# Hybrid decoder trunk on one core: the first two weight units run side by side over halves of the tokens, with smaller first loads, zero matmuls and a later sum of squares

## The reference

```python
def swiglu(x, w1, w3, w2):
    return (jax.nn.silu(x @ w1) * (x @ w3)) @ w2

def block(x, ...):
    x = x + 0.5 * rmsnorm(swiglu(rmsnorm(x, norm_g[0]), ffn1_w1, ffn1_w3, ffn1_w2), norm_g[1])
    mo, st = mixer(rmsnorm(x, norm_g[2]), w_in, ...)
    x = x + rmsnorm(mo, norm_g[3])
    x = x + 0.5 * rmsnorm(swiglu(rmsnorm(x, norm_g[4]), ffn2_w1, ffn2_w3, ffn2_w2), norm_g[5])
    return x, st
```

## Time and profile before

| | us |
|---|---|
| median of 3 runs | 1116.31 |
| lowest and highest of the 3 | 1115.22 and 1117.57 |
| the profiled execution's own time | 1118.76 |
| span of the profiled execution | 1116.7 |
| PE (matmul) busy | 1082.8 (97%) |
| PEld (weight load) busy | 1069.9 (96%) |
| DVE busy | 537.7 (48%) |
| ACT busy | 339.2 (30%) |
| POOL busy | 104.7 (9%) |
| mean granted TensorE clock | 0.985 of full speed |

### The profile page before, as it was taken

How to read it: one execution, slowest core, us unless ns; L and a number is a source line. 1 busy time by engine, 2 the same in 40 slices (tenths; PEclk the granted TensorE clock), 3 DMA queues, 4 the chain that set the end, 5 groups by cost and what they waited for, 6 DMA issues and landing times.

```text
span 1116.7 us, 21526 instructions
## 1 busy us (share of the span) xinstructions
PE 1082.8 (97%) x8929; PEld 1069.9 (96%) x8929; DVE 537.7 (48%) x942; ACT 339.2 (30%) x477; POOL 104.7 (9%) x175
## 2 busy tenths in 40 slices
PE   6999999999999999999999889999999999999995
PEld 6999999999999999998999789999999999999995
DVE  5534523433333369864546857844323334323346
ACT  5322213221222345411532333442212222113231
POOL 0000625910000000420001020000000000000000
PEclk9999999999999999999999989999999999999998
DMA  6222223233222240132312335122232232232232
GB/s 232 83 88 94 78 92 95 75 94 91 80 80 90 71 138 23 57 92 78 114 60 77 12 83 200 37 78 91 79 94 83 87 94 81 89 94 78 82 85 81
DMA packets 31921, 97.97 MB, mean 88 GB/s; under 512 B 5880, under 2 KB 8184, under 8 KB 31864
## 3 DMA queue, kind: packets, MB, share of 16 engines
q1 hardware_dynamic: 31864, 97.17, 28.8%
HBM read 92.46 MB, written 4.70 MB: 87 GB/s over the span
## 4 chain that ended last, share of the span: by engine, by line
PE 90%; DVE 6%; ACT 2%; DMA 1%; issue 1%; SPq 0%; DVEq 0%; ACTq 0%
PE ps L1855 76%; PE ps L1880 5%; PE ps L2283 2%; PE ps L1946 2%; DMA raw<-w 1%; PE ps L1892 1%; DVE x L1090 1%; PE ps L1887 1%; DVE y L1086 1%; DVE wl L896 1%; ACT wh L485 1%; PE ps L2134 0%; DVE xl L1095 0%; DVE xl L1509 0%; PE ps L2093 0%
## 5 line engine op out<-in xcount | busy, mean ns | idle before, releaser
L896 DVE TENSOR_TENSOR wl<-raw,wh 128x1024 fp32r<-128x1024 f32 (+1 forms) x149 | 183.1, 1229 | 467.5 <-ACT wh L485 467.2
L1855 PE MATMUL ps<-xh,wh 128*128 128x272 f32 x1680 | 350.9, 290 | 11.0 <-DVE xl L1005 10.8
L1855 PE MATMUL ps<-xl,wh 128*128 128x272 f32 x1680 | 348.4, 289 | 0.0
L1855 PE MATMUL ps<-xh,wl 128*128 128x272 f32 x1680 | 347.2, 288 | 0.0
L485 ACT CAST wh<-raw 128x1024 fp32r<-128x1024 f32 (+1 forms) x149 | 154.7, 1039 | 448.0 <-PE ps L1855 440.9
L1855 PEld LDWEIGHTS ps<-xh,wh 128*128 128x128 f32 x1680 | 264.3, 189 | 12.5 <-issue 11.7
L1855 PEld LDWEIGHTS ps<-xl,wh 128*128 128x128 f32 x1680 | 265.5, 189 | 0.0
L1855 PEld LDWEIGHTS ps<-xh,wl 128*128 128x128 f32 x1680 | 264.3, 189 | 0.0
L1855 PE MATMUL ps<-hh,wh 128*128 128x272 f32 x608 | 126.3, 289 | 0.5 <-DVE hl L917 0.5
L1855 PE MATMUL ps<-hl,wh 128*128 128x272 f32 x608 | 125.4, 287 | 0.0
L1855 PE MATMUL ps<-hh,wl 128*128 128x272 f32 x608 | 125.3, 287 | 0.0
(11 more groups left out here) (444 smaller groups left out, 1098.5 us busy)
## 6 DMA issues: line engine op xcount, KB each, us to landing
raw<-w SPq DMA_DIRECT2D x120, 512.0 KB, 3.5
raw<-win SPq DMA_DIRECT2D x25, 512.0 KB, 3.6
raw<-w SPq DMA_DIRECT2D x16, 384.0 KB, 3.1
raw<-wout SPq DMA_DIRECT2D x8, 512.0 KB, 3.6
x<-xT SPq DMA_DIRECT2D x4, 544.0 KB, 6.1
o_yT<-x SPq DMA_DIRECT2D x16, 136.0 KB, 1.7
cs<-cT SPq DMA_DIRECT2D x4, 516.0 KB, 4.5
o_sC<-cs SPq DMA_DIRECT2D x4, 516.0 KB, 6.8
```

The source lines that it names most:

```text
L896: V.tensor_tensor(wl[par][:, 0:cols], raw[par][:, 0:cols], wh[par][:, 0:cols].bitcast(F32), ALU.subtract).then_inc(split_done, 1)
L1855: last = mm(ps[:, bank + s, 0:HALF], w[:, kk * P:(kk + 1) * P], a[:, kk, s * HALF:(s + 1) * HALF], start=(kk == 0 and i == 0), stop=(kk == ...
```

## The change

- **Loads.** The first halves of units 0 and 1 (blocks `kk` 0 to 3), then their second halves, are loads of their own, of 128 x 512. `x` comes in six parts that keep the two halves of the tokens apart: block 0, block 1, blocks 2 and 3, blocks 4 to 7 of the first 272 tokens, then blocks 0 to 3 and 4 to 7 of the second. The first half of unit 0 is issued first. Units 2 and 3 are now loaded before the loop, and the further parameters (`prm`, `cst2`, `bst`) come after them, so behind SP's waits for the low parts of units 0 and 1.
- **ACT and DVE.** High and low parts are taken piece by piece, in the order in which the pieces are used. The table for the square root is loaded before the first cast.
- **PE, units 0 and 1.** `first_pair` replaces two calls of `up`: for the first half of the tokens, for each `kk`, three matmuls of unit 0 and three of unit 1; then the same for the second half.
- **PE, zeros.** Four matmuls of 128 x 272 on the cleared buffer `cbd`, in plain 32-bit, stand before that and wait only for the clearing.
- **Squares and sums.** On ACT the eight squares stand behind the cast of unit 2, on DVE the adds behind its low part. On PE the sums move from behind unit 1 to the first block of unit 3, and the spread from before the fourth block of unit 2 to before the third block of unit 3.

```diff
+X_PARTS = ((0, 0, 1), (0, 1, 2), (0, 2, 4), (0, 4, 8), (1, 0, 4), (1, 4, 8))
+X_WITH = ((0, 1, 2, 2, 3, 3, 3, 3), (4, 4, 4, 4, 5, 5, 5, 5))
...
+            first(0, 0, first_in[0])
             spe.dma_start(prm[:, gains], A["prm"][:, gains]).then_inc(gain_in, 16)
-            spe.dma_start(x[:, 0:2], A["xT"][:, 0:2]).then_inc(x_in[0], 16)
-            load(0, 0, A["w13_0"][0])
-            for i in range(1, 4):
-                spe.dma_start(x[:, 2 * i:2 * i + 2], A["xT"][:, 2 * i:2 * i + 2]).then_inc(x_in[i], 16)
-                if i == 1:
-                    spe.dma_start(cst[:], A["cst"]).then_inc(cst_in, 16)
-            load(1, 1, A["w13_0"][1])
+            x_part(0)
+            x_part(1)
+            first(1, 0, first_in[1])
+            x_part(2)
+            first(0, 1, raw_full[0])
+            first(1, 1, raw_full[1])
+            x_part(3)
+            x_part(4)
+            x_part(5)
+            spe.dma_start(cst[:], A["cst"]).then_inc(cst_in, 16)
+            load(2, 0, A["w13_0"][2])
+            load(3, 1, A["w13_0"][3])
...
                     elif f == 0:
-                        split(u0, u0 % 2, half(0))
-                        inputs(lambda: split(u0 + 1, (u0 + 1) % 2, half(1)))
+                        inputs()
                         split(u0 + 2, u0 % 2, half(2))
+                        for kk in range(KD):
+                            input_square(kk)
+                        split(u0 + 3, (u0 + 1) % 2, half(3))
                         input_root(0)
-                        split(u0 + 3, (u0 + 1) % 2, half(3))
                         input_copy(0, bcs[:])
...
                     elif f == 0:
-                        lo_part(u0, u0 % 2)
                         inputs()
-                        lo_part(u0 + 1, (u0 + 1) % 2)
+                        lo_part(u0 + 2, u0 % 2)
                         sum_squares(0)
-                        lo_part(u0 + 2, u0 % 2)
+                        lo_part(u0 + 3, (u0 + 1) % 2)
                         input_scale(0)
-                        lo_part(u0 + 3, (u0 + 1) % 2)
                         dve.wait_ge(r_copied, 1)
...
+            def first_pair():
+
+                for s in range(2):
+                    for kk in range(KD):
+                        pe.wait_ge(xl_ready, KD * s + kk + 1)
+                        for c in range(2):
+                            if s == 0 and kk == 0:
+                                pe.wait_ge(first_lo, c + 1)
+                            if s == 0 and kk == KD // 2:
+                                pe.wait_ge(split_done, c + 3)
+                            for i, (w, a) in enumerate(((wh, xh), (wh, xl), (wl, xh))):
+                                ins = mm(ps[:, 2 * c + s, 0:HALF], w[c][:, kk * P:(kk + 1) * P], a[:, kk, part(s)],
+                                         start=(kk == 0 and i == 0), stop=(kk == KD - 1 and i == 2))
+                            if s == 1 and kk == KD - 1:
+                                ins.then_inc(unit_used, 1)
...
-                        up(u0, hb, 0, lambda kk: pe.wait_ge(xl_ready, 2 * kk + 2))
-                        up(u0, hb, 1)
-                        input_sums(KD)
-                        up(u0, hb, 2, lambda kk: input_spread(0) if kk == 3 else None)
-                        up(u0, hb, 3)
+                        first_pair()
+                        up(u0, hb, 2)
+                        pe.wait_ge(cst_in, 16)
+                        up(u0, hb, 3, lambda kk: input_sums(KD) if kk == 0 else input_spread(0) if kk == 2 else None)
...
-            pe.wait_ge(cst_in, 16)
+            pe.wait_ge(warm_in, 1)
+            zeros = cbd[:].rearrange("p n j c -> p (n j c)")
+            for n in range(4):
+                mm(ps[:, 7, 0:HALF], zeros[:, 0:P], zeros[:, P:P + HALF], start=True, stop=True)
             ffn(0, 0, 0, 0)
```

More of the change, by code:

```diff
@@ L323, in build @@
         prm_in = sem("prm_in")
-        x_in = [sem(f"x_in{i}") for i in range(4)]
+        warm_in = sem("warm_in")
+        first_in = [sem(f"first_in{i}") for i in range(2)]
+        first_hi = sem("first_hi")
+        first_lo = sem("first_lo")
+        x_in = [sem(f"x_in{i}") for i in range(len(X_PARTS))]
         cs_in = sem("cs_in")
@@ L604, in input_square, with first_cast, inputs @@
                 nc.scalar.activation(sq_slot(kk), x[:, kk], ACT.Square).then_inc(xsq_ready, 1)
-            def inputs(between):
-                for kk in range(KD):
-                    x_loaded(kk)
-                    nc.scalar.activation(xh[:, kk], x[:, kk], ACT.Copy, scale=norm_g[:, 0, kk:kk + 1]).then_inc(xh_ready, 2)
-                between()
-                for kk in range(KD):
-                    input_square(kk)
+            def first_cast(u, z, full, done):
+                act.wait_ge(full, 16)
+                cut = slice(z * UNIT // 2, (z + 1) * UNIT // 2)
+                nc.scalar.copy(wh[u][:, cut], raw[u][:, cut]).then_inc(done, 1)
+            def inputs():
+                act.wait_ge(split_done, 2)
+                sqrt_table()
+                first_cast(0, 0, first_in[0], first_hi)
+                act.wait_ge(gain_in, 16)
+                for h in range(2):
+                    for kk in range(KD):
+                        act.wait_ge(x_in[X_WITH[h][kk]], 16)
+                        nc.scalar.activation(xh[:, kk, part(h)], x[:, kk, part(h)], ACT.Copy, scale=norm_g[:, 0, kk:kk + 1])\
+                            .then_inc(xh_ready, 1)
+                        if h == 0 and kk == 0:
+                            first_cast(1, 0, first_in[1], first_hi)
+                        if h == 0 and kk == 3:
+                            first_cast(0, 1, raw_full[0], hi_done)
+                            first_cast(1, 1, raw_full[1], hi_done)
             def input_root(stage):
@@ L1230, in s5_scalars @@
                     V.reciprocal(par(IDEN), par(S0)).then_inc(s5_par, 1)
-            def x_loaded(kk):
-                if kk == 0:
-                    dve.wait_ge(gain_in, 16)
-                dve.wait_ge(x_in[kk // 2], 16)
             def ffn1_inputs():
                 settle()
-                for kk in range(KD):
-                    x_loaded(kk)
-                    input_lo(kk)
+                first_low(0, 0, first_hi, 1, first_lo)
+                dve.wait_ge(gain_in, 16)
+                for h in range(2):
+                    for kk in range(KD):
+                        dve.wait_ge(x_in[X_WITH[h][kk]], 16)
+                        input_lo(h, kk)
+                        if h == 0 and kk == 0:
+                            first_low(1, 0, first_hi, 2, first_lo)
+                        if h == 0 and kk == 3:
+                            first_low(0, 1, hi_done, 1, split_done)
+                            first_low(1, 1, hi_done, 2, split_done)
             ffn(0, 0, 0, 0, ffn1_inputs, s5_scalars)
```

31 lines of the change are left out of this document (19 added, 12 removed).

## The result

The changed kernel takes **1125.85 us** (median of 5 runs, 1125.32 to 1127.16) against 1116.31 (5 runs): ratio 1.0078 [1.0059, 1.0096], 9.5 us slower. Two later groups of 6 runs each of the same kernel gave 1127.35 and 1127.68. Slower was forecast, at 1121.2; the measured time lies 0.85 us above the upper end of the range, 1125. The profiled execution took 1125.57 us, 6.8 more than that of before.

A forecast was written before the change was run, and what follows sets the result against it. TensorE, busy 97% of the span, was taken as the bound, so only its idling and lower clock count. Unit 4 later 2.3, clock after it 1.7, clock fall at unit 2 0.9: +4.9, 1121.2 us; range 1117.4 to 1125.

The forecast's parts named there:

- TensorE's start: At the kernel's start: first matmul of zeros at about 2.2 us, first matmul of `xh` at about 6.
- The end of the pair: Units 0 and 1 end at 19.0 us instead of 24.6, 5.6 won; bounds 17.9 and 20.6.
- the line of 403 KB per us: Loads at the start: each lands at 3.35 us plus the KB issued so far over 403.
- rival (D): Loads at the start: small pieces run at half rate, units 0 and 1 end at about 24; 1126 us, chance 0.06.
- The wait before unit 2: TensorE waits 2.0 us for unit 2's cast and low part, since both buffers stay in use; unit 2 starts at 21.0.
- The wait behind unit 2: TensorE waits 0.8 us, from unit 2's end at 27.0 to unit 3's low part at 27.8, before the sums.
- The wait before unit 4: TensorE waits 5.1 us for DVE's 9.5 us chain; unit 4 starts at 41.7 instead of 39.37, 2.3 later.
- The clock: After the wait before unit 4 the clock falls to half speed, 1.7 us lost; bounds 1.4 and 3.1.
- This goes through to the end: From unit 4 on TensorE is the bound in the same order, so the +4.9 us stays unchanged to the end.
- Rival (A): Start and waits: the clock holds and units 0 and 1 end at 18; 1117.5 to 1118.5 us, chance 0.13.
- (B): Before unit 4: DVE's chain has hidden slack, so no wait comes and the kernel is faster, 1113.5 us; chance 0.07.
- (C): Behind unit 2: the sums run at the half clock, costing 2.6 us in place of 0.9; 1123 us, chance 0.12.

The follow-up runs named there:

- e2: The change with the first block of small S5 steps on DVE moved from ahead of unit 4's low part to one call later: 1121.80 us, ratio 1.0047.
- e3: The change without the four matmuls of zeros and the wait for the clearing: 1125.13 us, ratio 1.0090.
- e4: The change with `x` loaded in five parts over all 544 tokens, runs of 2176 bytes instead of 1088: 1126.57 us, ratio 1.0089.
- e12: The change with units 0 and 1 loaded whole, runs of 4096 bytes instead of 2048: 1127.15 us, ratio 1.0088.
- e1: The change with squares, adds, sums and spread back where they stood in the kernel before: 1119.34 us, ratio 1.0020.
- a3: The change run again unaltered for a third trace, 6 runs: unit 4 starts at 45.47 us, and 1082.1 us from there to the end.
- e6: The kernel before with fourteen matmuls of zeros put in front of unit 0: 1114.45 us, ratio 0.9980.
- b1: The kernel before run again unaltered for a second trace, 12 runs: unit 4 starts at 39.60 us, and 1074.4 us from there to the end.

## Why the prediction was wrong, and what of it held

- **TensorE's start.** Zeros at 2.20, `xh` at 6.08; forecast 2.2 and about 6. Right.
- **The end of the pair.** 21.1 against 19.0, and beyond the bound of 20.6. **This step failed.** The term was the line of 403 KB per us. It was taken from loads of 512 and 544 KB, and the 350 of the constants was asked of the `x` parts alone, as 0.4 us in all. Measured are 270 to 289 GB/s from 4 to 8 us, against the 413 of the line. The landing of `x` blocks 4 to 7 came 1.75 late, and `xl` stood 1.2 behind it and not 0.95. Short runs explain a part of the low rate; the rest of its cause is open. With 1.75 us in 9.05, rival (D) was half right; by its price, half the rate, the part would have landed at 14. The Trainium skill, "DMA: Bandwidth & Descriptors", section Bandwidth, asks for loads of 1 MiB or more to reach 75% of the peak. The trace bears this out for the small parts, which ran at about two thirds of what the large ones carried, and not for the large ones: 512 and 544 KB are below 1 MiB too, and carried 406 to 419 GB/s.
- **The wait before unit 2.** 2.08 against 2.0. Right.
- **The wait behind unit 2.** 0.8 was forecast, if unit 2 ran at the full clock. By the prediction's own sum it is a wait for the low part of unit 3, for the adds end before unit 2 does. In the change the stretch at 1.2 GHz took its place, as the 0.9 in the sum allowed: the low part was done at 30.09, and PE was through unit 2 and began the sums at 30.99. In e2, e3, e4 and e12, where the clock held in unit 2, the wait is there, with 0.55 to 0.57. Right.
- **The wait before unit 4.** 5.0 against 5.1; from the end of the pair to unit 4 it was 23.6 us in the forecast with the 0.9, and 23.7 in the trace. Together with e1 and e2 the mechanism stands: both buffers held to the end of the pair, the adds behind the cast, and DVE's chain of 9.5 us without its cover.
- **The clock.** A fall behind the wait in front of unit 4 was forecast at 1.7 us. From unit 4 to the first down projection the three traces of the change take 1.5 to 1.9 us longer than those of before. a3's stretch at 1.2 GHz is twice as long, 6.8 us, but 3.0 of it lie in the wait and cost nothing. Right.
- **"This goes through to the end."** The second step that fell short. Some 2.4 us were lost in stretches at 1.2 GHz far behind the change. The prediction put this at nothing, though the earlier trace rows show such stretches there. Why the change has more of them stays open.

The two add up: at unit 4 the forecast was +3.2 (2.3 + 0.9), the mean of the traces +5.4, nearly all of the difference from the end of the pair; then 1.7, forecast and seen; then 2.4 on the mean. That is 9.5 instead of 4.9. The range failed twice: the pair ended 0.5 us beyond its bound, and nothing was set aside for the clock far behind. That the median still came within 1 us of the upper end is luck: the bounds for the clock and the sums, 2.25 us in all, were not needed and covered the rest.

Rival (A) falls, for the start was not early enough and the clock fell twice. (B) falls by the wait of 5.0 and by e2: the chain in front of unit 4 had no slack. (C) did not come about in the change, whose spread took 1.41 us; in e3 and e4 it took 2.57, at half the clock.

## What to carry to other kernels

An early start is worth what the waits behind it leave. Here 3.5 us were won in the pair, and more than that was lost by holding both weight buffers to its end and by moving a sum behind a cast: an engine that is busy 48% of the span had a chain with 0.2 us of slack to the bound one. Before a reduction is moved later, follow its result to the next weights and count the slack there. And take the rate of small loads from small loads.

The best kernel measured is e6, the old order with matmuls of zeros in front: 1114.45 us, 0.20% [0.07, 0.34] below before, about what can be told from no change.

## What the runs showed that was not expected

- The same busy share of the DMA engines carried different rates: a DMA share of 1.00 was 270 GB/s with parts of 136 to 272 KB, and 1.03 was 406 GB/s with parts of 512 and 544.
- Time at 1.2 GHz came in stretches at places that differ between executions of one kernel: 17.1 to 23.9 us in three traces of before. That is a scatter of some 3 us of time, more than most terms of this case.
- The granted clock also fell where PE waited for nothing: in b1 at 530 right behind 3.7 us of matmuls whose operands fill 4 of 128 partitions, in a3 at 541 within the same matmuls.
- The same four zeros were followed by the full clock from 8.03 on in the change, with a wait of 0.66 us behind them, and not before 14 in e12 (1.38) and e4 (0.82 and 0.44). In those two the pair ended 2 us later.
- Fourteen matmuls of zeros that ran 0.7 us past the moment at which unit 0 could have begun (11.49 against 10.77) still made it end 0.9 us sooner (23.73 against 24.67).
